# A twelve-sublayer transformer kernel: the identity matmuls between sublayers 4 to 11 are taken out

## The chip, the cores and the metric

The kernel runs on one core of one Trainium2 chip, as one launch. The metric is the device time of that launch in microseconds (us), as the median of a few executions. TensorE (PE in the rows) does the matmuls, VectorE (DVE), ScalarE (ACT) and GpSimd (POOL) the elementwise work, and SyncE (SP) issues the transfers.

## What is computed

The reference is two small transformer stacks of two layers each, one behind the other, on 256 tokens of width 1024 (the first stack also carries 256 context tokens). A layer has three sublayers: a gated feed-forward, a mixer (differential attention, neighbourhood attention, windowed attention with a pooling branch, a convolution with a state-space scan), and another feed-forward. Each sublayer stands between two norms:

```python
x = x + 0.5 * rms_norm(swiglu(rms_norm(x, nw[0]), w_gate, w_up, w_down), nw[1])
hn = rms_norm(x, nw[2])
m = even_mixer(hn, ...)
x = x + rms_norm(m, nw[3])
x = x + 0.5 * rms_norm(swiglu(rms_norm(x, nw[4]), ...), nw[5])
```

In the first stack the norm before a sublayer is also shifted and scaled, and the norm behind it gated, by vectors that come from a conditioning input times the matrices `ada_w`.

## The kernel before

The activations stand transposed: 1024 features are 8 tiles of 128 partitions, the tokens lie along the free axis (512 columns up to sublayer 3, 256 after that). The residual `h` and everything between sublayers stays in on-chip memory. Weights are streamed from HBM by SP in chunks of up to 1 MB into a ring of four raw buffers. A product of 32-bit accuracy is made of three fast ones: ACT rounds a chunk to its high part (`make_high`, line 304), DVE subtracts it for the rest (`make_rest`, line 316), and PE multiplies high by high, high by rest and rest by high (`products`, lines 333 to 335).

The sublayers have the numbers 0 to 11. The work is written out by hand, one program for each engine, and only semaphores order the engines against each other; a feed-forward's chunks run in a loop. The place that matters here is the **hand-over** from one sublayer to the next, written in the TensorE program at the end of `build_program`. It has these steps:

1. PE adds up the squares of the sublayer's output, over partitions, with matmuls by a matrix of ones (`out_pe`, lines 667 and 670). ACT takes the root (line 420), DVE the reciprocal (line 425).
2. DVE scales the 8 output tiles (`post_dve`, line 529); POOL (line 542) and DVE (line 525) add them to the residual.
3. ACT squares each residual tile (line 453), PE sums the squares in the same way (`pre_pe`, which calls `sum_squares`, line 414), ACT takes the root again, DVE the reciprocal.
4. DVE scales each tile (line 509), ACT rounds it (line 464 or 466), DVE or POOL makes its rest (line 481 or 484), and PE starts on the first chunk of the next sublayer tile by tile.

Behind sublayers 0 to 3 PE has products of the conditioning matrices to do during a hand-over (`mod_products`, line 352); `behind(s)` says which. Behind sublayers 4 to 10 there are none, and there PE runs matmuls whose result nobody reads:

```python
WARM = 18, 16
def keep_warm(n):
    for _ in range(n):
        nc.tensor.matmul(bank[3][:, 0:P], ident[:], ident[:], start=True, stop=True)
```

Eighteen stand between steps 1 and 3, sixteen between steps 3 and 4. They wait for nothing, and nothing waits for them but what stands behind them in PE's own queue. A matmul of 32-bit operands shows as two records in the trace, so a hand-over has 68 of line 433.

Of the kernel before, what the change touches and what calls it, by code (L numbers as in the profile page):

```python
# [1 line left out]

# [11 lines left out]
P = 128  # L26
# [20 lines left out]
NEG = -1e9  # L47
FAR = -1e30
RAW_RING, PART_RING = 4, 2
WARM = 18, 16  # L50
POOL_RESTS = [2, 5]
DVE_ADDS = [2, 5, 7]

# [71 lines left out]
def build_program(nc, t, out):  # L125
# [3 lines left out]
    for name, _, _, n, cols in plan:  # L129
        first_chunk[name] = len(chunk_cols)  # L130
        chunk_cols += [cols] * n

    parted = [g for name, _, _, n, _ in plan if not name.startswith("ada")
              for g in range(first_chunk[name], first_chunk[name] + n)]
    part_of = {g: q for q, g in enumerate(parted)}
    columns, n_columns = param_columns()
    subs = list(range(12))

    with ExitStack() as ctx:
        top = [(nc.sbuf_base + 31) // 32 * 32]  # L140

        def place(name, shape, dt, offset=None):

            size = (int(np.prod(shape[1:])) * 4 + 31) // 32 * 32
            where = top[0] if offset is None else offset
            if offset is None:
                top[0] += size
            assert where + size <= nc.sbuf_usable_end, (name, where + size, nc.sbuf_usable_end)
            return nc.alloc_sbuf_tensor_at(name, shape, dt, offset=where)
# [36 lines left out]
        bank = [ctx.enter_context(nc.psum_tensor(f"bank{n}", [P, 512], F32)) for n in range(8)]  # L186
# [48 lines left out]
        def width_in(s):  # L235
            return BOTH if s <= 4 else SEQ
# [9 lines left out]
        def round_h(s):  # L246
            return 2 * s + 2
# [6 lines left out]
        def behind(s):  # L254

            if s == subs[-1]:
                return []
            return {0: [(0, 3), (0, 4)], 1: [(1, 0), (1, 1)], 2: [(1, 2), (1, 3)], 3: [(1, 4), (1, 5)]}.get(s, [])
# [82 lines left out]
        def mod_products(layer, m, steps=range(4)):  # L341

            pe = nc.tensor
            g0, q = first_chunk[f"ada{layer}_{m}"], ada_index[f"ada{layer}_{m}"]
            for j in steps:
                g = g0 + j
                pe.wait_ge(raw_landed[g % RAW_RING], 16 * (g // RAW_RING + 1))
                if j == 0 and q:
                    pe.wait_ge(mod_read, q)
                c = CHUNK * (j % 2)  # L350
                for kt in range(KT):
                    ins = pe.matmul(mod[0:4, c:c + CHUNK], cond4[:, j // 2, kt, :],  # L352
                                    raw[:, g % RAW_RING, kt * CHUNK:(kt + 1) * CHUNK],
                                    start=j == 0 and kt == 0, stop=j == 3 and kt == KT - 1)
                ins.then_inc(w_used, 1)
# [6 lines left out]
        def mod_turn(layer, m):  # L362

            nc.tensor.wait_ge(mod_copied, ada_index[f"ada{layer}_{m}"] + 1)
            for k in range(KT // 2):
                ins = nc.tensor.transpose(mod[:, 4 * k:4 * k + 4], mod_rows[:, k * P:(k + 1) * P], ident[0:4, 0:4])
            ins.then_inc(mod_turned, 1)
# [58 lines left out]
            nc.vector.wait_ge(rinv_ready, q + 1)  # L426

        eps_col = small[:, 0:1]

        def keep_warm(n):  # L430

            for _ in range(n):
                nc.tensor.matmul(bank[3][:, 0:P], ident[:], ident[:], start=True, stop=True)

        def load_table(func):

# [4 lines left out]
        def pre_pe(q, n):  # L441
            for kt in range(KT):
                sum_squares(q, kt, n)
# [108 lines left out]
        def ffn_in_pe(s):  # L552
            pe = nc.tensor
            g0, n, f = first_chunk[f"in{s}"], width_in(s), FT * (s // 3 * 2 + (s % 3 == 2))

            def body(j, i):
                g = g0 + j
                await_parts(g, i)
                if j >= 2:
                    pe.wait_ge(gate_done, at(f + j - 1, RAW_RING, i))  # L560
                if j == 0:
                    for kt in range(KT):
                        await_u(pe, s, kt)
                        for m in range(2):
                            ins = products(bank[2 * m][:, 0:n], g, [kt], lambda w, k: block_of(w, g, k, m),
                                           lambda k: uhi[:, k, 0:n], lambda k: ulo[:, k, 0:n],
                                           first=kt == 0, last=kt == KT - 1)
                else:
                    for m in range(2):
                        ins = products(bank[2 * m + j % 2][:, 0:n], g, range(KT), lambda w, k: block_of(w, g, k, m),  # L570
                                       lambda k: uhi[:, k, 0:n], lambda k: ulo[:, k, 0:n])
                ins.then_inc(w_used, 1)

            ring_loop(pe, FT, body)
# [54 lines left out]
        def tiles_of(s, j):  # L629

            _, per, _ = out_shape(s)
            return [j // 2] if per == -2 and j % 2 else [] if per == -2 else list(range(per * j, per * (j + 1)))
# [105 lines left out]
        def ffn_out_pe(s):  # L738
            f = FT * (s // 3 * 2 + (s % 3 == 2)) + FT

            def ready(j):
                nc.tensor.wait_ge(glo_done, f if j else f - HALF_FT)

            out_pe(s, lambda k, n: ghi[:, k, 0:n], lambda k, n: glo[:, k, 0:n], ready)
# [282 lines left out]
        ident = place("identity", [P, P], F32)  # L1027
# [842 lines left out]
        @block.sync  # L1870
        def _(sp):
            sp.dma_start(par[:], t["params"]).then_inc(par_landed, 16)
            sp.dma_start(ident[:], t["identity"]).then_inc(par_landed, 16)
            for name, src, row, n, cols in plan:
                g0 = first_chunk[name]
                for j in range(n):
                    load_chunk(sp, name, src, row, g0, j, None)
                    s = {("in1", 5): 1, ("in4", 5): 4, ("in7", 5): 7, ("in10b", 1): 10}.get((name, j))
                    if s in mixers:

                        sp.wait_ge(w_used, first_chunk[f"in{s}"])
                        mixers[s].loads(sp)
                if name == "ada0_0":
                    sp.dma_start(h[:], t["tokens"]).then_inc(in_landed, 16)
            last = subs[-1]

            for kt in range(KT):
                await_h(sp, last, kt)
                sp.dma_start(out[:, kt], h[:, kt, 0:out.shape[2]]).then_inc(out_done, 16)
            sp.wait_ge(out_done, 16 * KT)  # L1890
# [88 lines left out]
        @block.tensor  # L1979
        def _(pe):  # L1980
            pe.wait_ge(const_ready, 3)
            pe.wait_ge(par_landed, 32)
            pe.wait_ge(cond_ready, 2)
            mod_products(0, 0)
            mod_turn(0, 0)
            mod_products(0, 1)
            pre_pe(0, BOTH)
            mod_turn(0, 1)
            mod_products(0, 2)
            mod_turn(0, 2)  # L1990
            for s in subs:
                if s in mixers:
                    mixers[s].pe(pe)
                    mixers[s].out(pe)
                else:
                    ffn_in_pe(s)
                    ffn_out_pe(s)
                groups = behind(s)
                if groups:
                    mod_products(*groups[0], range(2))  # L2000
                elif s != subs[-1]:
                    keep_warm(WARM[0])
                if s != subs[-1]:
                    pre_pe(round_h(s), width_in(s + 1))
                    if not groups:
                        keep_warm(WARM[1])
                if groups:
                    mod_products(*groups[0], range(2, 4))
                    mod_turn(*groups[0])
                    mod_products(*groups[1])  # L2010
                    mod_turn(*groups[1])
# [175 lines left out]
```

## Time and profile before

| | |
|---|---|
| three timed runs | 3482.84, 3483.27, 3486.34 us |
| median | 3483.27 us |
| profiled execution, first to last instruction (its span) | 3481.2 us |
| what lies around the span, taken against the median | 2.1 us |
| PE busy in the span | 3312.5 us (95%) |
| DVE, ACT, POOL busy | 1657.4 (48%), 1226.6 (35%), 391.6 (11%) us |
| mean granted TensorE clock | 0.973 |
| bytes read from HBM | 429.46 MB, 124 GB/s over the span |

No total time is listed for the profiled execution apart from its span; the span lies 2.1 us under the median of the timed runs. Engines overlap, so their busy times don't add up to the span. A granted clock of 1.00 is 2.4 GHz, 0.50 is 1.2 GHz. A matmul's record is longer than its turn on the array, because matmuls are pipelined: the time from one start to the next is its cost in a dense stretch.

### The profile page before, as it was taken

To read this page: it belongs to the slowest core of one execution; us is meant where nothing else is said; L and a number is where in the kernel's file an instruction comes from. 1 tells how busy PE (TensorE), PEld (TensorE's weight loads), DVE (VectorE), ACT (ScalarE), POOL (GpSimd) and SP (SyncE) were. 2 spreads that over 40 slices of the span, in tenths; PEclk is the share of its full clock that TensorE was granted. 3 is DMA by queue.
4 is the path that set the end of the run, shared out by engine and by line. 5 is a ranking of instruction groups with operands and counts; after the bars stand their busy time and mean duration, and the time that the engine had idled before them with its cause. 6 is when DMAs were issued, how large, how long until landed. Compare 5 with 4: busy or idle time off the path is not lost.

```text
span 3481.2 us, 47424 instructions
## 1 busy us (share of the span) xinstructions
PE 3312.5 (95%) x19602; PEld 2735.6 (79%) x19602; DVE 1657.4 (48%) x2233; ACT 1226.6 (35%) x1821; POOL 391.6 (11%) x308
## 2 busy tenths in 40 slices
PE   7999989988999999999899999999999999978998
PEld 3888848645688857888485699999679999976898
DVE  3332253475433244332523564555665464697654
ACT  2222232352322223222323444444444444344443
POOL 0000110001000110001120100101010100393201
PEclk9999999999999999999999999999789999989999
DMA  6222332331422242223532244445225544430453
GB/s 249 92 97 80 107 137 87 119 109 64 144 97 87 93 152 93 97 79 111 193 111 97 98 144 165 163 172 182 75 73 182 181 147 168 160 108 19 142 176 122
DMA packets 66683, 432.72 MB, mean 124 GB/s; under 512 B 7392, under 2 KB 8928, under 8 KB 26976
## 3 DMA queue, kind: packets, MB, share of 16 engines
q1 hardware_dynamic: 66528, 430.54, 35.3%
q8 instruction: 111, 1.82, 0.2%
q14 instruction: 44, 0.36, 0.0%
HBM read 429.46 MB, written 1.05 MB: 124 GB/s over the span
## 4 chain that ended last, share of the span: by engine, by line
PE 85%; DVE 11%; ACT 3%; issue 1%; DMA 0%; POOL 0%; SPq 0%; DVEq 0%; ACTq 0%
PE bank L333 22%; PE bank L334 22%; PE bank L335 22%; PE bank L352 7%; DVE sublayer_out L529 3%; PE bank L906 2%; PE bank L930 2%; DVE w_rest L316 2%; DVE work_b L425 1%; PE bank L915 1%; PE bank L834 1%; DVE work_a L509 1%; PE bank L836 1%; PE bank L835 1%; DVE od_glu L1506 1%
## 5 line engine op out<-in xcount | busy, mean ns | idle before, releaser
L333 PE MATMUL bank<-u_high,w_high 128*128 128x256 f32 (+1 forms) x3392 | 1110.8, 327 | 50.6 <-DVE u_rest L481 28.9
L334 PE MATMUL bank<-u_rest,w_high 128*128 128x256 f32 (+1 forms) x3392 | 1103.9, 325 | 0.0
L335 PE MATMUL bank<-u_high,w_rest 128*128 128x256 f32 (+1 forms) x3392 | 1103.6, 325 | 0.0
L316 DVE TENSOR_TENSOR w_rest<-w_raw,w_high 128x2048 fp32r<-128x2048 f32 (+2 forms) x366 | 754.3, 2061 | 643.2 <-ACT w_high L304 643.1
L304 ACT ACTIVATE w_high<-w_raw 128x2048 fp32r<-128x2048 f32 (+3 forms) x371 | 635.3, 1712 | 513.3 <-PE bank L335 459.8
L333 PEld LDWEIGHTS bank<-u_high,w_high 128*128 128x128 f32 x3392 | 655.2, 193 | 110.1 <-DVE u_rest L481 24.1
L335 PEld LDWEIGHTS bank<-u_high,w_rest 128*128 128x128 f32 x3392 | 655.2, 193 | 50.2
L334 PEld LDWEIGHTS bank<-u_rest,w_high 128*128 128x128 f32 x3392 | 655.5, 193 | 49.5
L333 PE MATMUL bank<-gated_high,w_high 128*128 128x256 f32 (+1 forms) x1408 | 454.9, 323 | 1.8 <-DVE w_rest L316 1.8
L334 PE MATMUL bank<-gated_rest,w_high 128*128 128x256 f32 (+1 forms) x1408 | 454.4, 323 | 0.0
L335 PE MATMUL bank<-gated_high,w_rest 128*128 128x256 f32 (+1 forms) x1408 | 454.4, 323 | 0.0
L593 ACT ACTIVATE work_a<-bank 128x256 f32<-128x256 f32 (+1 forms) x176 | 81.7, 464 | 854.0 <-PE bank L335 853.9
L618 DVE TENSOR_TENSOR work_b<-work_a,bank 128x256 f32<-128x256 f32 (+1 forms) x176 | 91.7, 521 | 556.3 <-ACT work_a L593 556.3
L333 PEld LDWEIGHTS bank<-gated_high,w_high 128*128 128x128 f32 x1408 | 268.0, 190 | 23.4 <-DVE w_rest L316 2.8
L334 PEld LDWEIGHTS bank<-gated_rest,w_high 128*128 128x128 f32 x1408 | 268.0, 190 | 20.6
L335 PEld LDWEIGHTS bank<-gated_high,w_rest 128*128 128x128 f32 x1408 | 268.0, 190 | 20.5
L684 POOL TENSOR_TENSOR work_a<-squares 128x256 f32<-128x256 f32 (+1 forms) x12 | 23.7, 1973 | 2263.5 <-ACT squares L401 2263.5
L352 PE MATMUL bank<-w_raw,cond_silu 128*4 128x256 f32 x1152 | 261.3, 385 | 13.5 <-DMA w_raw<-in_w_ada 7.3
L352 PEld LDWEIGHTS bank<-w_raw,cond_silu 128*4 128x4 f32 x1152 | 97.8, 88 | 180.2 <-issue 42.9
L687 POOL TENSOR_TENSOR work_a<-work_a,squares 128x256 f32<-128x256 f32 (+1 forms) x57 | 110.2, 1934 | 385.6 <-ACT squares L401 384.7
L947 ACT ACTIVATE attn_exp<-bank,attn_columns 128x512 f32<-128x512 f32 (+1 forms) x120 | 70.0, 586 | 124.6 <-DVE attn_columns L994 82.7
L725 DVE COPY sublayer_out<-bank 128x256 f32<-128x256 f32 (+1 forms) x64 | 31.4, 506 | 149.6 <-PE bank L335 149.6
(229 smaller groups left out, 3282.1 us busy)
## 6 DMA issues: line engine op xcount, KB each, us to landing
w_raw<-in_w_ffn_in SPq DMA_DIRECT2D x176, 1024.0 KB, 4.8
w_raw<-in_w_ffn_out SPq DMA_DIRECT2D x128, 704.0 KB, 4.0
w_raw<-in_w_ada SPq DMA_DIRECT2D x72, 1024.0 KB, 4.8
w_raw<-in_w_mix SPq DMA_DIRECT2D x58, 1024.0 KB, 4.8
w_raw<-in_w_od_out SPq DMA_DIRECT2D x8, 768.0 KB, 4.4
na_bias<-in_na_bias SPq DMA_DIRECT2D x1, 4096.0 KB, 14.2
residual<-in_tokens SPq DMA_DIRECT2D x1, 2048.0 KB, 16.0
ev_const<-in_ev_const SPq DMA_DIRECT2D x1, 1280.0 KB, 7.5
```

The source lines that it names most:

```text
L304: nc.scalar.activation(whi[:, q % PART_RING, 0:n], raw[:, g % RAW_RING, 0:n], ACT.Copy)\
L316: eng.tensor_tensor(wlo[:, q % PART_RING, 0:n], raw[:, g % RAW_RING, 0:n], whi[:, q % PART_RING, 0:n].bitcast(F32), ALU.subtract).then_inc ...
L333: pe.matmul(ps, hi, a, start=first and n == 0, stop=False)
L334: pe.matmul(ps, hi, b, start=False, stop=False)
L335: ins = pe.matmul(ps, lo, a, start=False, stop=last and n == len(kts) - 1)
L352: ins = pe.matmul(mod[0:4, c:c + CHUNK], cond4[:, j // 2, kt, :], raw[:, g % RAW_RING, kt * CHUNK:(kt + 1) * CHUNK], start=j == 0 and kt = ...
L529: ins = dve.scalar_tensor_tensor(y[:, kt, sl], y[:, kt, sl], G[:, s, kt, c:c + 1], rinv[:, sl], ALU.mult, ALU.mult)
L593: act.activation(ta[:, j % 2, 0:n], bank[j % 2][:, 0:n], ACT.Silu).then_inc(silu_done, 1)
L618: dve.tensor_tensor(tb[:, j % 2, 0:n], ta[:, j % 2, 0:n], bank[2 + j % 2][:, 0:n], ALU.mult)\
L687: pool.tensor_tensor(ta[:, 0, 0:n], ta[:, 0, 0:n], sq[:, d % 2, 0:n], ALU.add)\
L906: pe.matmul(bank[m % 4][:, 0:it["keys"]], q, k, start=True, stop=True)\
L947: act.activation(attn_e[:, m % 4, 0:it["keys"]], bank[m % 4][:, 0:it["keys"]], ACT.Exp, bias=attn_cols[:, 0, m:m + 1], accum_out=attn_cols ...
```

## The change

The helper `keep_warm`, its two calls in each hand-over, and the constant `WARM` are gone. The twelve empty lines at the head of the file that go too only move line numbers (line 414 is 401 in the changed file, 333 is 320).

```diff
-WARM = 18, 16
...
-        def keep_warm(n):
-
-            for _ in range(n):
-                nc.tensor.matmul(bank[3][:, 0:P], ident[:], ident[:], start=True, stop=True)
...
                 groups = behind(s)
                 if groups:
                     mod_products(*groups[0], range(2))
-                elif s != subs[-1]:
-                    keep_warm(WARM[0])
                 if s != subs[-1]:
                     pre_pe(round_h(s), width_in(s + 1))
-                    if not groups:
-                        keep_warm(WARM[1])
                 if groups:
                     mod_products(*groups[0], range(2, 4))
                     mod_turn(*groups[0])
```

On PE, in the hand-over behind sublayer 4 (neighbourhood attention, whose last products are the `na_o` rows), before:

```order
4884 L667 MATMUL bank<-work_a,ones 128x256
4885 L670 MATMUL bank<-squares,ones 128x256 x2
4886 L433 MATMUL bank<-identity 128x128 x18
4887 L414 MATMUL bank<-squares,ones 128x256 x8
4888 L433 MATMUL bank<-identity 128x128 x16
4889 L333 MATMUL bank<-u_high,w_high 128x256
```

and in the changed kernel:

```order
4884 L649 MATMUL bank<-work_a,ones 128x256
4885 L652 MATMUL bank<-squares,ones 128x256 x2
4886 L401 MATMUL bank<-squares,ones 128x256 x8
4887 L320 MATMUL bank<-u_high,w_high 128x256
```

The two rows of the identity are gone and nothing else has moved. It is the same at all seven places: 14 rows fewer on PE, and the rows of DVE, ACT, POOL and SP are the same but for their line numbers.

## Rows read from the trace of the kernel before

**Rows 1.** The page: granted clock in 40 slices of the span; chain by engine.

```profile
PEclk9999999999999999999999999999789999989999
...
PE 85%; DVE 11%; ACT 3%; issue 1%; DMA 0%; POOL 0%; SPq 0%; DVEq 0%; ACTq 0%
```

**Rows 2.** Instructions of line 433: count, min/median/max ns, first and last start.

```profile
L433 PE MATMUL bank<-identity x476: 272/275/275, 2004.4 to 3275.4; 128*128 128x128 f32 x159
```

**Rows 3.** Timeline of PE, hand-over 4 to 5: start, us, instruction, [idle before <-releaser].

```profile
2003.40 1.13 PE L670 MATMUL bank<-squares,ones 128*128 128x256 f32 x4 [0.53 <-ACT squares L401]
2004.37 4.18 PE L433 MATMUL bank<-identity 128*128 128x128 f32 x36
2008.90 0.70 PE L414 MATMUL bank<-squares,ones 128*128 128x256 f32 x2 [0.35 <-ACT squares L453]
...
2012.23 2.64 PE L414 MATMUL bank<-squares,ones 128*128 128x256 f32 x8 [0.56 <-ACT squares L453]
2014.71 3.73 PE L433 MATMUL bank<-identity 128*128 128x128 f32 x32
2019.27 0.36 PE L333 MATMUL bank<-u_high,w_high 128*128 128x256 f32 x1 [0.82 <-DVE u_rest L481]
```

**Rows 4.** Chain that ended last, in the same hand-over: start, us, what.

```profile
2006.93 2.61 DVE sublayer_out L529 x4
...
2013.67 1.78 DVE w_rest L316
2015.45 0.34 issue
2015.79 1.76 DVE work_b L425
...
2018.63 0.50 DVE u_rest L481
```

**Rows 5.** Windows: length, busy of PE PEld DVE ACT POOL, PEclk, DMA, GB/s.

```profile
2008.90:2014.60 5.70, 4.92 (x16) 2.48 (x17) 5.67 (x9) 2.92 (x7) 2.94 (x4) 1.00 0.00 0
2014.60:2018.50 3.90, 3.84 (x34) 3.63 (x32) 3.82 (x4) 0.88 (x2) 0.00 (x0) 1.00 0.41 111
...
2019.30:2025.50 6.20, 6.20 (x49) 6.09 (x50) 5.06 (x13) 4.51 (x8) 0.00 (x0) 1.00 0.11 45
```

**Rows 6.** Windows, PE alone: first, last and sum of twelve stretches around long waits.

```profile
48.90:50.70 1.80, 0.05 (x1) 1.00 0.00 0
...
3218.40:3221.70 3.30, 0.82 (x5) 1.00 0.00 0
sum 34.50, PE 3.58; mean PE 0.30
```

**Rows 7.** Windows, PE alone: the twelve stretches of low clock that follow those.

```profile
50.80:57.50 6.70, 5.53 (x14) 0.50 0.00 0
...
3221.80:3225.10 3.30, 3.30 (x14) 0.50 0.01 2
sum 53.40, PE 47.97; mean PE 4.00
```

**Rows 8.** Timeline of PE, first chunk of sublayer 4, low clock up to 1726.7.

```profile
1723.57 0.41 PE L334 MATMUL bank<-u_rest,w_high 128*128 128x256 f32 x1
1723.78 0.41 PE L335 MATMUL bank<-u_high,w_rest 128*128 128x256 f32 x1
...
1726.86 0.28 PE L334 MATMUL bank<-u_rest,w_high 128*128 128x256 f32 x1
1726.98 0.28 PE L335 MATMUL bank<-u_high,w_rest 128*128 128x256 f32 x1
```

**Rows 9.** Timeline of PE in sublayer 10: the same eight records at either clock.

```profile
3206.90 1.51 PE L1820 MATMUL bank<-od_maps,od_x_tokens 128*64 128x256 f32 x8 [1.28 <-DVE od_maps L1743]
...
3212.08 2.82 PE L1820 MATMUL bank<-od_maps,od_x_tokens 128*64 128x256 f32 x8 [3.04 <-DVE od_maps L1743]
```

**Rows 10.** Windows of all engines: attention of sublayer 7.

```profile
2481.10:2552.60 71.50, 68.41 (x203) 38.22 (x204) 44.75 (x170) 31.93 (x122) 0.00 (x0) 0.50 0.00 1
```

## The prediction

> **What bounds the kernel now.** The page first: PE holds 85% of the chain that ended last, and its clock stands at 9 tenths or more in all slices but three [rows 1]. So the kernel is as long as its matmuls, and its rest is the places where PE has to wait for DVE and ACT. The hand-overs are such places, and the change touches nothing else. That sets two questions: is any of the work that goes on the path, and does the clock of the work behind it depend on it?
>
> The instructions of line 433 come next: 476 records from 2004.4 to 3275.4 us, 7 hand-overs of 68 [rows 2]. The timeline shows where they lie in the first of the seven [rows 3]. PE ends the sums of the output's squares at 2003.40 + 1.13 = 2004.53, runs 36 records of the identity up to 2008.55, and still waits 0.35 us for ACT's first square at 2008.90. The sums of the residual's squares end at 2012.23 + 2.64 = 2014.87; 32 records of the identity lead up to 2018.44, and PE again waits 0.82 us, for the first rest of DVE at 2019.27. The six others have the same steps at the same distances, within 0.3 us. The chain through this stretch runs over DVE: scaling the output, the rest of a weight chunk, the reciprocal, the first rest [rows 4]. No step of it waits for line 433.
>
> **The work removed: 0 us.** 36 + 32 records an average of 0.116 us apart (4.18 us for 36) are 7.9 us for each hand-over, 55 us in all, and every one lies inside a wait for DVE or ACT, with 0.35 and 0.82 us to spare. PE's queue reaches the next matmul earlier, but its operand comes no sooner. The cover of this zero is the chain of rows 4; nothing is gained unless it becomes shorter, and the change does nothing to it. The matmuls' own bank is read by no one, and no transfer, semaphore or buffer hangs on them.
>
> **What PE does instead: it stands still twice.** Without line 433 it idles from 2004.53 to 2008.90, 4.4 us, and from 2014.87 to 2019.27, 4.4 us, seven times each. In the whole trace of before there are twelve waits of PE over 2.2 us that begin at full clock, 2.2 to 3.7 us long, all at places where line 433 doesn't stand. All twelve are followed by a fall to 0.50, that is 1.2 GHz, in the wait or within 2.2 us of its end (the first and the last of them, with their clock, in [rows 6]; the low stretches that follow in [rows 7]). Of six between 2.0 and 2.2 us four were followed by one. In the seven hand-overs, which have PE busy nearly throughout, the clock is 1.00 from end to end [rows 5]. Waits of 4.4 us are longer than any of the twelve, so I take it that both waits of each hand-over let the clock fall.
>
> **What the fall costs behind the second wait.** The twelve low stretches last 3.3 to 6.8 us and 53.4 us together, 4.45 each, of which PE is busy 47.97, or 4.0 [rows 7]. The rest of them lies before PE resumes or in further waits. I take 4.3 us of low clock on the products of the next sublayer; the ends are 2.8 us (the fall comes early in the wait) and 6.8. The price of a low microsecond: the first chunk's matmuls start 0.21 us apart at the low clock and 0.12 apart at the full one [rows 8], so 1 - 0.12/0.213 = 44% of the time is lost: 4.3 x 0.44 = 1.89 us. Some comes back: the first chunk's 48 matmuls take 6.2 us [rows 5] where 48 x 0.12 = 5.76 would do, since DVE's rests come one by one. PE behind its operands can use that 0.45 us. From the second chunk on PE is dense and waits for nobody, so the remaining 1.44 us stay. DVE, ACT and the transfers can run ahead meanwhile, but PE has no later wait in a feed-forward in which to catch up.
>
> The Trainium skill ("TensorE: Matmul & The Clock Gate", What's actually happening, and Terms) says that the slow clock is the default, which activity lifts, and that a low stretch costs its length times (1 - K/N), here a half. By that factor the term would be 4.3 x 0.5 - 0.45 = 1.70 us, and the whole sum 1.8 us larger than mine; the rows' 0.21 against 0.12 bear out the direction, with a slightly smaller price.
>
> **What the fall costs behind the first wait.** The eight sums of squares would run at the low clock at first. Eight records of another 32-bit product take 2.82 us low and 1.51 full [rows 9], nearly double. A tile's two records of 256 columns are about 0.44 us of PE at full, from 0.116 us for one record of the identity's 128 columns [rows 3], so about 0.87 low. All eight low would be 7.0 us from 2008.90, ending at 2015.9 where now it is 2014.87: 1.0 us late. But DVE's reciprocal waits for the rest of the weight chunk that stands before it, not for the root: the chain passes through line 316 and 0.34 us of issue, and begins line 425 at 2015.79 [rows 4], 0.4 us after ACT has its root. So the path gets 0 to 0.6 us. Dense low work lifts the clock again within one short stretch in most of rows 7, so mostly the later tiles catch up: 0.12 us.
>
> **The sum.** Seven hand-overs x (1.44 + 0.12) = 10.9 us. The span goes from 3481.2 to 3492.1, and with the 2.1 us around it, which is how the span stands to the median, the time is 3483.3 + 10.9 = 3494.2 us. Ends: 7 x (2.8 x 0.44 - 0.45) = 5.5 us, and 7 x (6.8 x 0.44 - 0.45 + 0.6) = 22 us. The seven hand-overs meet the clock at different moments, so neither end will hold for all seven: I take 8 to 15 us, and the spread of the runs of before, 3.5 us, on top.
>
> **Rivals.**
>
> *The clock stays up (chance 0.10, 3483 us).* For it: two waits of about 2.1 us passed without a fall, and the sums of squares stand between the two waits. Against it: twelve of twelve waits over 2.2 us. A fall in the second wait alone would still cost some 10 us, so for no change neither may fall. That the change doesn't do what it says comes out here too, and the order of PE's instructions rules it out: 14 rows gone, nothing else moved.
>
> *Low throughout (0.08, 3502 us).* The clock falls in the first wait, is not lifted by the sums, which have pauses at full clock but hardly any at half, and stays down through the second wait and for 6.8 us of products, with the root 0.4 us late: 6.8 x 0.44 - 0.45 + 0.2 = 2.7 us, seven times, 19 us. Four of the twelve low stretches were of the long kind.
>
> *The attention of sublayer 7 gets the full clock (0.06, 3467 us), the other side.* It now runs at 0.50 for 71.5 us after a wait, PE busy 68.4 of it, DVE 44.8 and ACT 31.9 [rows 10]. It is the one place where half clock lasts. The hand-overs behind sublayers 4 to 6 would move its start against the clock's steps by some 5 us. If it then ran at full clock, DVE would bound it: up to 71.5 - 44.8 = 27 us gained, 16 net of the 10.9 lost. From 11 us gained there the kernel is faster than before. For it: the work there is nearly dense at half clock, so the rise can't be far. Against it: in 71.5 us it never came, whatever part of the pattern it met, and the waits of DVE that let the clock fall are still there.
>
> In the main case the falls within sublayers 7 and 10 may shift as well; that is part of the spread.
>
> **Chances and range.** Forecast 0.76, low throughout 0.08, clock stays up 0.10, sublayer 7 0.06. A measurement of this kernel tells 0.2%, about 7 us, from no change: above 3490.2 us counts as slower, below 3476.3 as faster. Of the forecast's 0.76 some 0.06 lie under 3490.2. So slower 0.70 + 0.08 = 0.78, same 0.10 + 0.06 = 0.16, faster 0.06. The range from 3487 to 3501 us holds nearly all of the forecast and the lower edge of the low-throughout case, about 0.8.
>
> **What the changed profile would show.** Line 433's records gone; in each of the seven hand-overs two waits of PE of 4.3 to 4.5 us, named for ACT's squares and DVE's rest. Granted clock 0.50 in some part of each, and for 3 to 7 us behind the resumption, with line 333's equivalents 0.21 us apart. The hand-over itself, from the last output product to the first product of the next sublayer, 17.0 us as now, or up to 0.6 more. The first chunk 1 to 2.5 us longer than 6.2; later chunks and sublayers 0 to 3 unchanged. Wrong, if hand-overs show 1.00 throughout; if the waits are shorter than 4 us, which would mean that line 433 did hold something up; or if the difference lies in sublayers 7 and 10 and not in the first chunks.

## The result and the profile after

The changed kernel takes 3495.48 us (median of 6 runs, 3494.32 to 3497.82) against 3483.06 us (median of 6, 3482.38 to 3486.63) for the kernel before in the same session: 12.4 us more. The ratio taken over all runs is 1.0033, with a 95% interval of 1.0021 to 1.0044. The forecast was 3494.2 us in a range of 3487 to 3501. The profiled execution spans 3493.1 us, 11.9 more than before.

The page of the changed kernel, beside [rows 1] of before:

```profile
PE 3279.4 (94%) x19126; PEld 2708.1 (78%) x19126; DVE 1654.6 (47%) x2233; ACT 1226.9 (35%) x1821; POOL 393.7 (11%) x308
...
PEclk9999999999999999999999999999779999989999
...
PE 85%; DVE 11%; ACT 2%; issue 1%; DMA 0%; POOL 0%; SPq 0%; DVEq 0%; ACTq 0%
```

PE has 476 records fewer (19126 against 19602) and is busy 33 us less, and the kernel is longer. Its mean granted clock is 0.961 where it was 0.973. The row of the page by slices shows hardly any of this: the hand-overs are short.

The timeline of PE in the hand-over from sublayer 4 to 5 of the changed kernel answers to [rows 3] (start, us, instruction, [idle before <-releaser]; line 401 is 414 before, 320 is 333):

```profile
2004.22 1.13 PE L652 MATMUL bank<-squares,ones 128*128 128x256 f32 x4 [0.53 <-ACT squares L388]
2009.72 6.03 PE L401 MATMUL bank<-squares,ones 128*128 128x256 f32 x16 [4.37 <-ACT squares L435]
2020.08 0.55 PE L320 MATMUL bank<-u_high,w_high 128*128 128x256 f32 x1 [4.33 <-DVE u_rest L463]
2020.43 0.41 PE L321 MATMUL bank<-u_rest,w_high 128*128 128x256 f32 x1
2020.64 0.41 PE L322 MATMUL bank<-u_high,w_rest 128*128 128x256 f32 x1
```

The two waits are there, 4.37 and 4.33 us, and behind the second the products start 0.21 us apart, as in the low stretch of [rows 8]. The sums of squares, which came in groups with pauses between them, now make one stretch of 6.03 us. The hand-over as such has not become longer: from the first of the last sums of the output's squares to the first product it takes 2020.08 - 2004.22 = 15.86 us, before 2019.27 - 2003.40 = 15.87. The chain that ended last goes over DVE as in [rows 4]:

```profile
2014.49 1.84 DVE w_rest L303
2016.33 0.28 issue
2016.61 1.75 DVE work_b L412
...
2019.45 0.49 DVE u_rest L463
```

The windows of the same hand-over (length, busy of PE PEld DVE ACT POOL, granted clock, DMA share, GB/s), beside [rows 5]:

```profile
2005.35:2009.72 4.37, 0.01 (x2) 0.01 (x1) 3.72 (x5) 2.69 (x3) 1.40 (x2) 0.76 0.00 0
2009.72:2015.75 6.03, 6.03 (x16) 4.31 (x16) 6.00 (x9) 2.92 (x7) 2.94 (x4) 0.61 0.00 0
2015.75:2020.08 4.33, 0.00 (x1) 0.04 (x1) 4.12 (x6) 1.38 (x3) 0.00 (x0) 0.74 0.52 191
2020.10:2024.60 4.50, 4.50 (x21) 4.50 (x22) 4.50 (x12) 2.82 (x6) 0.00 (x0) 0.50 0.11 47
2024.70:2028.00 3.30, 3.30 (x29) 3.30 (x29) 0.48 (x1) 1.62 (x3) 0.00 (x0) 1.00 0.02 5
```

The clock falls inside the first wait, is back at the end of the sums, falls again inside the second, and stays low for the first 4.5 us of products: 21 records where a window of 3.3 us at full clock has 29. At all seven places there are two low stretches, one for each wait. Thirteen of the fourteen falls come inside the wait or at its end; the second one of the fifth hand-over comes 0.6 us behind the first product (2809.72 against 2809.10 us). The next rows are windows of PE alone over the low stretches: the second ones of the first, fourth and sixth hand-over, and the sum over all fourteen:

```profile
2017.90:2024.60 6.70, 4.52 (x21) 0.50 0.38 149
...
2598.10:2604.90 6.80, 5.60 (x26) 0.50 0.27 114
...
3018.00:3021.30 3.30, 3.30 (x16) 0.50 0.26 107
...
sum 70.40, PE 59.43; mean PE 4.24
```

Where the 11.9 us of the span went can be read by matching PE's other instructions one to one in the two traces. From the start of a hand-over (the last sums of the output's squares) to 60 records behind the first product, the changed kernel takes longer by

| hand-over behind sublayer | 4 | 5 | 6 | 7 | 8 | 9 | 10 | sum |
|---|---|---|---|---|---|---|---|---|
| first product later by, us | 0.0 | 0.0 | 0.4 | 0.25 | 0.0 | 0.0 | 0.0 | 0.6 |
| behind the first chunk later by, us | 1.6 | 1.1 | 2.5 | 2.3 | 1.1 | 1.1 | 1.0 | 10.8 |
| low behind the first product, us | 4.6 | 3.4 | 5.8 | 5.6 | 3.4 | 3.4 | 3.3 | 29.5 |

The rest is 0.8 us by which this execution was late before the first of these hand-overs, where both kernels are the same program, 0.7 us less in sublayer 7, 1.6 us more in sublayer 10, and 0.5 us less at the end: 10.8 + 0.8 - 0.7 + 1.6 - 0.5 = 12.0. The 1.6 us in sublayer 10 can't be put down to the change: in the two traces below whose hand-overs are those of before, the same part moved by +1.6 and by -1.0 us.

### The profile page after: what moved, and what is told of

The parts are those of the page before. It is cut to its first block, busy times and chain, and to the rows that moved or that the text cites. A ratio compares the mean times of both kernels' runs of the same rounds, so it can differ in the third digit from the quotient of the medians.

```text
span 3493.1 us, 46472 instructions
## 1 busy us (share of the span) xinstructions
PE 3279.4 (94%) x19126; PEld 2708.1 (78%) x19126; DVE 1654.6 (47%) x2233; ACT 1226.9 (35%) x1821; POOL 393.7 (11%) x308
## 4 chain that ended last, share of the span: by engine, by line
PE 85%; DVE 11%; ACT 2%; issue 1%; DMA 0%; POOL 0%; SPq 0%; DVEq 0%; ACTq 0%
PE bank L320 22%; PE bank L321 22%; PE bank L322 22%; PE bank L339 7%; DVE sublayer_out L511 2%; PE bank L888 2%; PE bank L912 2%; DVE w_rest L303 2%; PE bank L897 1%; DVE work_b L412 1%; PE bank L816 1%; DVE work_a L491 1%; PE bank L818 1%; PE bank L817 1%; DVE od_glu L1488 1%
## 5 line engine op out<-in xcount | busy, mean ns | idle before, releaser
L401 PE MATMUL bank<-squares,ones 128*128 128x256 f32 (+1 forms) x192 | 86.7, 591 | 44.2 <-ACT squares L435 44.0
```

Source lines behind the costliest of these rows:

```text
L401: pe.matmul(stat[:, 0:n], ones[:], slots(sq, n)[1](kt), start=kt == 0, stop=kt == KT - 1)\
```

## The experiments

Theory: the identity matmuls cost nothing where they stand and hold the granted clock; without them it falls in the waits, and the products behind the second wait pay. The rivals are in each expectation. Each kernel is the kernel before with one number or a few lines changed, but for the first of the last group, which starts from the changed kernel.

### One wait at a time

```diff
-WARM = 18, 16
+WARM = 0, 16
```

> The sixteen matmuls behind the sums of squares stay, the eighteen ahead of them are taken out. Clock theory: the clock falls in each of the seven first waits, the sums of squares start at 0.50, and the clock is back before the sixteen start or soon after, so that the products of the next sublayer begin at 1.00. What is left is a late root: 0 to 0.5 us for each hand-over, 0.5 us in all on average, at most 4: 3483.5 to 3487 us. Rival A, each of the two waits costs its share alike: half of the 12.4 us, 3489 us. Rival B, the matmuls of the identity do something other than hold the clock (the first product after a wait is slow to start): the same half.

```diff
-WARM = 18, 16
+WARM = 18, 0
```

> The eighteen stay, the sixteen behind the sums are taken out. Clock theory: nearly the whole loss comes back, since the clock falls in the second wait and the first chunk of the next sublayer runs at 0.50 for 3.4 or 6.8 us: 10 to 12.5 us more than before, 3493 to 3496 us. The first wait shows 1.00. Rival A (half for each wait): 3489 us.

| kernel | us | ratio to before, 95% interval |
|---|---|---|
| the sixteen alone (0, 16) | 3483.08 | 0.9998 (0.9989 to 1.0007) |
| the eighteen alone (18, 0) | 3493.08 | 1.0031 (1.0019 to 1.0043) |
| before, same session | 3483.55 | |

Within the noise the whole loss belongs to the second wait. Windows of the kernel with the sixteen alone, its first hand-over:

```profile
2006.00:2012.70 6.70, 4.42 (x10) 3.25 (x11) 6.63 (x12) 3.08 (x8) 4.35 (x5) 0.50 0.00 0
2012.80:2018.60 5.80, 5.03 (x39) 4.56 (x37) 5.58 (x7) 1.80 (x4) 0.00 (x0) 1.00 0.39 127
2018.70:2025.00 6.30, 6.30 (x50) 6.20 (x51) 5.04 (x13) 4.54 (x8) 0.00 (x0) 1.00 0.11 43
```

The clock does fall in the first wait or at its end, for 3.4 or 6.8 us at each of the seven places, and this costs nothing: in no hand-over is the first product later by more than 0.02 us. The sums run at half clock for a while, end late by less than DVE's own delay, and the clock is up before the sixteen. With the eighteen alone it is the reverse. Two windows of PE in its first hand-over, from the eighteen to the last sum and from the fall to its end:

```profile
2001.30:2011.50 10.20, 9.12 (x54) 1.00 0.05 21
2014.50:2021.20 6.70, 4.41 (x21) 0.50 0.39 148
```

Its seven hand-overs are longer by 1.6, 1.1, 2.3, 2.2, 1.5, 1.0 and 0.9 us, 10.6 in all. Rivals A and B both asked for about 3489 us from each of the two kernels; with 3483.08 and 3493.08 us both are refuted as they were priced. A milder form of B, in which the sixteen do something else for the first product, is answered by the rows: the loss behind the first product grows with the time at 0.50 there. Where 3.0 to 3.4 us were low it is 0.9 to 1.1 us, where 4.2 to 4.6 were low 1.5 to 1.6, and where 5.6 to 6.1 were low 2.1 to 2.3, over the fourteen hand-overs of this kernel and of the changed one.

### Half as many

```diff
-WARM = 18, 16
+WARM = 9, 8
```

> Nine and eight matmuls in place of 18 and 16: PE then stands still for about 2.4 us in the first wait and 2.6 in the second. By the twelve waits over 2.2 us of the trace of before, all followed by a fall, every hand-over still falls: 3493 to 3496 us. By a model in which a fall also depends on when the wait comes, some of the seven fall and some don't: 2 to 9 us more than before, 3488 us likeliest. Rival (any matmul in the wait is enough): 3483 us.

3485.91 us, ratio 1.0006 (0.9997 to 1.0015). The times alone don't tell this from no change; the trace does. The waits are 2.3 to 2.6 us now. The timeline of PE in its fifth hand-over:

```profile
2786.41 2.17 PE L433 MATMUL bank<-identity 128*128 128x128 f32 x18
2790.87 0.70 PE L414 MATMUL bank<-squares,ones 128*128 128x256 f32 x2 [2.29 <-ACT squares L453]
...
2796.69 1.95 PE L433 MATMUL bank<-identity 128*128 128x128 f32 x16
2801.09 0.36 PE L333 MATMUL bank<-u_high,w_high 128*128 128x256 f32 x1 [2.45 <-DVE u_rest L484]
```

and two windows of PE, that fifth hand-over and the seventh:

```profile
2786.00:2801.00 15.00, 9.57 (x52) 1.00 0.35 117
3262.00:3277.90 15.90, 10.85 (x54) 0.89 0.31 107
```

In the first, second, third and seventh hand-over both waits led to a fall, and each cost 1.0 to 1.1 us; in the fourth only the first wait did, at no cost; in the fifth and sixth the clock stayed at 1.00, again at no cost. The sum over the seven is 4.2 us. So waits of the same length and the same surroundings go either way, and the prediction's reading of its twelve waits, that a wait over 2.2 us is followed by a fall, doesn't hold at 2.3 to 2.5 us. At 3.9 to 4.4 us it held 14 times of 14. The Trainium skill ("TensorE: Matmul & The Clock Gate", What's actually happening) says that the chip's watch over PE's activity runs on freely and doesn't begin anew with the kernel's work, so that the same work meets it at another moment in another run; the seven hand-overs of this one execution agree with that.

### What the matmuls cost once they are on the path

```diff
-WARM = 18, 16
+WARM = 18, 30
```

> Eighteen and thirty: 14 more matmuls behind the sums, 14 x 0.232 = 3.25 us of PE, of which 0.7 to 0.8 us is idle now. If the chain through DVE is what ends the wait, PE starts the next sublayer 2.4 to 2.5 us late in each hand-over, of which 0.45 to 0.5 us comes back in the first chunk: 7 x 2.0 = 14 us more (12 to 17), 3495 to 3500 us. This prices the matmuls once they are on the path. Rival (the matmuls already lie on the path, so that taking them out gained something that the clock hid): each of the 14 costs its full 0.232 us, 7 x 3.25 = 23 us, 3506 us, and the 16 that stood there gave back about 26 us when they went.

3493.93 us, 10.4 us more than before, ratio 1.0028 (1.0017 to 1.0039). The chain of its first hand-over:

```profile
2013.86 0.70 PE bank L414 x2
2014.55 6.70 PE bank L433 x60
```

Line 433 is now on it. In each hand-over the first product comes 2.06 to 2.23 us late, and 1.69 to 1.84 us are left behind the first chunk, 12.6 us in all; 0.8 us less in sublayer 7 makes up part of the difference to the median. Of the 3.25 us added 1.0 to 1.2 fit into the wait, the rest delays the first product in full, and the first chunk gives back 0.4 us of it. The median moved by less than the expected 12 to 17 us, and both it and the trace's 12.6 us are far from the rival's 23. So the sixteen were not on the path, and a filled wait has an upper end: here 14 too many cost about as much as none at all.

### The attention of sublayer 7

The stage that runs at 0.50 for 71.5 us [rows 10] was a rival in the prediction. It begins with waits of 1.1, 0.8 and 2.1 us. The next two kernels are the kernel before with the same kind of matmul there, into a bank whose last reader in this sublayer ends at 2457.4 us, well ahead of them:

```diff
+EV_WARM = 3, 9, 10, 0
...
                 for t_ in (6, 7):
+                    ev_warm(EV_WARM[0])
                     rope_pe(self.r0, t_, t_, self.q, self.rope[:, 0:P], self.proj.base + 4 + t_ + 1)
+                ev_warm(EV_WARM[1])
                 pe.wait_ge(rope_done, self.r0 + 8)
...
                         self.fill_pe(i)
+                        if self.kind == "ev":
+                            ev_warm(EV_WARM[2] if i == 2 else EV_WARM[3] if i > 2 else 0)
```

> The kernel before, with matmuls of the identity added in sublayer 7 alone: 3 ahead of each of the last two rotations, 9 ahead of the first scores, 10 behind the third scores, 25 in all, in the waits of 1.1, 0.8, 2.1 and 2.0 us at the start of its attention. If waits of PE are what lets the clock fall there, it starts the attention at 1.00. Then DVE, 44.8 us busy in the 71.5 us of that stage, or the chain of one map through DVE and ACT, bounds it: 18 to 25 us gained, 3458 to 3465 us. Rival: the matmuls of this attention, on 64 of 128 rows or columns, don't hold the clock by themselves once they are half as dense, and it falls again in the middle of the stage: 3 to 15 us gained, 3468 to 3480 us. Rival: the fall has nothing to do with these waits: 3483 us.

```diff
-EV_WARM = 3, 9, 10, 0
+EV_WARM = 3, 9, 10, 1
```

> The same with one more matmul of the identity behind the scores of each of the other 21 maps of sublayer 7. If the clock holds by itself in the kernel without them, these cost nothing as long as DVE is the bound (0.23 us each, 4.9 us in all, if PE is): 3458 to 3468 us. If the clock falls again in that kernel, this one is the faster of the two by up to 15 us: 3460 us against 3468 to 3480.

Without one for each map: 3481.10 us, ratio 0.9993 (0.9983 to 1.0002). With it: 3463.31 us, ratio 0.9941 (0.9924 to 0.9957), 19.8 us faster than the 3483.07 of before. The first has about the time of the second rival (3483 us) and yet the trace of the first one, a full clock at the start that falls again, without the 3 to 15 us of gain priced for it; the second beats the first by 17.8 us, more than the 15 that were expected at most. Windows of the kernel without:

```profile
2481.00:2500.00 19.00, 17.92 (x71) 10.33 (x68) 13.52 (x51) 8.63 (x35) 0.00 (x0) 0.66 0.00 0
2500.00:2520.00 20.00, 20.00 (x59) 10.83 (x59) 13.24 (x50) 8.71 (x35) 0.00 (x0) 0.50 0.01 1
```

and of the kernel with it:

```profile
2481.00:2500.00 19.00, 18.07 (x96) 11.06 (x94) 16.62 (x66) 11.40 (x47) 0.00 (x0) 1.00 0.00 0
2500.00:2520.00 20.00, 19.53 (x101) 11.93 (x100) 17.99 (x70) 11.80 (x48) 0.00 (x0) 1.00 0.00 1
```

The filled waits carried the full clock into the attention, but it fell at 2487.0 all the same, once the maps ran by themselves, and stayed down for 61 us. With one matmul more for each map it is 1.00 throughout, and sublayer 7 is 19.1 us shorter, counted from hand-over to hand-over. DVE, 17.99 of 20 us busy, is not what is left as the bound there. In the same 20 us the chain that ended last lies on PE; one map of it:

```profile
2503.39 0.63 PE bank L911 x2
2504.01 0.42 PE bank L438 x2
2504.43 0.08 issue
2504.51 0.41 PE bank L922 x2
2504.91 0.58 PE bank L937 x4
```

Line 438 is the added matmul. It holds 20.9% of this chain between 2500 and 2520 us, and 15.7% over the whole attention, where the largest step of DVE has 3.6%. So the filling is on the path here, and pays all the same; whether fewer of them would hold the clock was not tried.

That the waits ahead of the attention are all that keeps it at half clock is thereby refuted: it lost the full clock with them filled, behind waits of at most 1.1 us, and at half clock its own matmuls, most of them on 64 rows or 64 columns of the array, don't bring it back, with PE busy in all of 20 us. Whether it falls for the narrow matmuls, for the short pauses between them or for the transposes (line 922, 15.1 of the 61.4 us) was not tried apart.

### Both, and more of the same

```diff
+EV_WARM = 3, 9, 10, 1
...
-                elif s != subs[-1]:
-                    keep_warm(WARM[0])
...
-                    if not groups:
-                        keep_warm(WARM[1])
```

> The changed kernel (no identity matmuls in the seven hand-overs) with the identity matmuls in sublayer 7 of the kernel that ran at 3463 us. If the hand-overs' loss is local to them, it comes on top unchanged: 11 to 13 us more than that kernel, 3474 to 3476 us. If the two interact (a low clock that is carried from one place to the next), the sum fails by several us either way.

3475.21 us, ratio 0.9975 (0.9966 to 0.9985): 11.9 us above the 3463.31 of another session (11.5 if each is taken against its own before), and its seven hand-overs are longer than those of before by 10.9 us in the trace. The two effects add up, so the loss is local to each hand-over.

```diff
-WARM = 18, 16
+WARM = 0, 16
+EARLY = 12, 5
+EV_WARM = 3, 9, 10, 1
...
                     for kt in range(KT):
+                        if kt == 2 and g0 + 1 in rest_by_pool:
+                            early_warm(EARLY[0])
                         await_u(pe, s, kt)
...
                     mod_turn(*groups[1])
+                    early_warm(EARLY[1])
```

> The kernel that ran at 3463 us, with the eighteen of each hand-over left out and the sixteen kept, and identity matmuls at more places where PE waits over 1 us and the clock falls now: 12 behind the second step of the first chunk of sublayers 0 to 4, 5 ahead of the first step of sublayers 1 to 4. There are nine falls there, 3.4 or 6.8 us low, one of 10.2. If a fall costs 44% of the low time on products, less what comes back: 8 to 12 us gained, 3451 to 3456 us. If most of that low time lies in the wait for DVE's rests anyway: 0 to 5 us gained, 3458 to 3463 us. If the 12 matmuls (2.8 us) come late behind a low clock and hold PE: slower than 3463 us.

3464.99 us (3460.71 to 3470.82, 5 runs), ratio 0.9948 (0.9935 to 0.9962): no gain over the 3463.31 of the kernel without the early ones, against an expected 8 to 12 us, or 0 to 5. The falls in the first chunks behind sublayers 1 and 2 (at 890.4, 897.3, 1303.4 and 1310.3 us of the trace of before) are gone, and each of those two chunks is shorter by only 0.2 us. The timeline of PE in the second of them:

```profile
1301.97 2.84 PE L443 MATMUL bank<-identity 128*128 128x128 f32 x24
1306.55 0.50 PE L335 MATMUL bank<-u_high,w_high 128*128 128x512 f32 x1 [1.74 <-DVE u_rest L491]
```

PE is done with its two steps and with the filling and waits for DVE for 1.74 us more; what the full clock saves on PE goes into that wait. A fall costs where dense work follows, and these are followed by another wait. Behind sublayer 3 the chunk is 0.6 us longer: its low stretch, from 1716.5 to 1726.7 us before, is now from 1721.6 to 1728.4 and lies on products, not in a wait. The attention of sublayer 4, in which nothing was added, took 3.2 us longer in this execution, with 10.2 us of low clock in it where before it had 3.4. That hides what the early ones gain elsewhere, so this run doesn't price them all.

## Why the prediction was right

**The work removed costs nothing.** Held. PE's first product came neither earlier nor, in five of seven hand-overs, later; the kernel with more of them shows what they cost on the path. The prediction named waits under 4 us as a sign that line 433 had held something up, and two of the second waits are 3.87 us. They are short for another reason: the sums before them end 0.8 and 0.6 us late at the low clock.

**Two waits, two falls at each place.** Held 14 times of 14, with waits of 3.9 to 4.4 us. The evidence was read too widely, though: at 2.3 to 2.6 us, where the twelve waits of before also said "fall", it goes either way.

**The cost behind the second wait, 1.44 us.** 29.5 us low behind the first product over seven hand-overs, 4.2 each, where the forecast took 4.3. At 0.44 that is 1.85 us, less the 0.45 that the first chunk gives back: 1.4. Measured: 10.8 us less 0.6 for late first products, 1.46 each. The Trainium skill's factor ("TensorE: Matmul & The Clock Gate", Terms), a half of the low time, would give 4.2 x 0.5 - 0.45 = 1.65; the runs lie nearer to the rows' 44%, which have 0.21 us from start to start low against 0.12 full.

**The cost behind the first wait, 0.12 us.** Measured 0.09: 0.4 and 0.25 us in the two hand-overs in which the low stretch covered the sums up to their last 0.7 us, nothing elsewhere. In the third hand-over the timeline of all engines shows the mechanism, DVE now waiting for ACT's root and no longer for its own rest:

```profile
2434.88 0.47 ACT L407 ACTIVATE work_b<-bank,small 128x256 f32<-128x256 f32 x1 [1.57 <-PE bank L401]
...
2435.39 1.75 DVE L412 RECIPROCAL work_b<-work_b 128x256 f32<-128x256 f32 x1 [0.33 <-ACT work_b L407]
```

In the kernel with the sixteen alone this term is zero, but none of its seven low stretches reached so near to the end of the sums; in the changed kernel with the matmuls in sublayer 7 (3475.21 us) two did, and cost 0.42 and 0.36 us. So the term depends on when the fall comes, and its average of 0.12 us was a fair guess more than a derivation.

**The sum** was 10.9 us, the seven hand-overs of the trace have 10.8, and the median moved by 12.4. The rest of the traced difference lies in sublayer 10 and in the start, where kernels with the same hand-overs differ as much, and within the spread that the range allowed for. The low time behind the second wait came out at 29.5, 30.4 and 29.6 us in the three traces with that wait open, and the loss at 10.8, 10.6 and 10.9 us. The sum of seven is steadier than the single hand-over, so its agreement with the forecast is not the luck of one execution.

**The rivals.** "The clock stays up" and "low throughout" were each seen only in part: no fall in two hand-overs of the kernel with half as many, late sums in two of the changed one. "Sublayer 7 gets the full clock" had the wrong trigger: a shift in time did not bring it about in any of the kernels, one more matmul for each map did. Its bound of 27 us took DVE for what would be left; 19 us were gained, with PE still on the chain and the added matmuls in it.

## What to carry to other kernels

Price idle matmuls by what stands behind the wait: they pay where dense matmuls follow at once (1.5 us for each such wait here, for sixteen matmuls that cost nothing), and not where another wait or a slack of the neighbouring engine follows. Look in the windows of the trace for long stretches at half clock with a busy PE before trimming anything else; here one such stretch was worth more than all seven hand-overs. And count the filling against the wait: beyond its end each matmul costs its full time.

## What was not expected of the hardware

- PE busy 68.4 of 71.5 us, most of it with matmuls on 64 rows or columns, left the granted clock at 0.50 throughout, and the same stage, entered at 1.00, fell within 7 us of its first scores. One identity matmul of 128 rows and columns for each map of about 2 us held it at 1.00.
- Waits of 2.3 to 2.6 us in seven equal places: the clock fell in some of them and in others not, within one execution.
- Half clock around the sums of squares for 3.4 to 6.8 us cost nothing in seven of seven hand-overs of the kernel with the sixteen alone, since the engine behind them was late anyway. It cost 0.25 to 0.42 us in four of the fourteen hand-overs of the two kernels with both waits open.
